# Low parts of 30 second feed-forward weight blocks: a DMA that adds the weights onto a negated high part, in place of VectorE's subtraction

## The reference, cut to what matters

```python
# first block, feed-forward part
h = rms_norm(x, g_pre_mlp[layer]) * (1.0 + scale2) + shift2
f = jnp.square(jax.nn.relu(h @ w_fc1[layer])) @ w_fc2[layer]
x = x + gate2 * rms_norm(f, g_post_mlp[layer])
# second block
for layer in range(DEPTH_2):
    hn = rms_norm_2(h, norm_g[layer])
    ...
    h = h + y.astype(h.dtype)
return rms_norm_2(h, final_g)
```

## Time and profile before

| what | value |
|---|---|
| median of 3 runs | 1418.52 us (1418.33 to 1418.89) |
| profiled execution, device time | 1419.24 us |
| profiled execution, span | 1417.4 us |
| TensorE busy | 1401.6 us, 99% of the span |
| VectorE busy | 948.4 us, 67% |
| ScalarE busy | 606.8 us, 43% |
| GpSimd busy | 0.2 us |
| moved by DMA | 157.99 MB, mean 111 GB/s |

### The profile page before, as it was taken

How to read it: one execution, slowest core, us unless ns; L and a number is a source line. 1 busy time by engine, 2 the same in 40 slices (tenths; PEclk the granted TensorE clock), 3 DMA queues, 4 the chain that set the end, 5 groups by cost and what they waited for, 6 DMA issues and landing times.

```text
span 1417.4 us, 21825 instructions
## 1 busy us (share of the span) xinstructions
PE 1401.6 (99%) x8618; PEld 1195.4 (84%) x8618; DVE 948.4 (67%) x1886; ACT 606.8 (43%) x1176; POOL 0.2 (0%) x4
## 2 busy tenths in 40 slices
PE   8999989999999999999999999999999999999998
PEld 7888878999998888888888888888888888888886
DVE  7887777789963335756466535422788889888645
ACT  6423345555542324542332333433445545556441
POOL 0000000000000000000000000000000000000000
PEclk9999999999999999999999999999999999999999
DMA  9656453233332324022332233132222222221221
GB/s 352 221 186 251 156 198 116 75 106 119 104 120 92 102 92 161 31 104 90 104 104 74 94 116 134 60 104 89 75 91 74 91 76 75 76 75 61 76 75 60
DMA packets 43734, 157.99 MB, mean 111 GB/s; under 512 B 4849, under 2 KB 5233, under 8 KB 43633
## 3 DMA queue, kind: packets, MB, share of 16 engines
q1 hardware_dynamic: 43344, 156.39, 32.4%
q10 hardware_dynamic: 288, 0.21, 0.0%
HBM read 154.48 MB, written 2.10 MB: 110 GB/s over the span
## 4 chain that ended last, share of the span: by engine, by line
PE 96%; DVE 2%; DMA 1%; issue 0%; ACT 0%; SPq 0%; DVEq 0%; ACTq 0%
PE PS L584 27%; PE PS L586 27%; PE PS L585 27%; PE PS L925 3%; PE PS L927 3%; PE PS L926 3%; PE PS L1056 1%; PE PS L580 1%; PE PS L1060 1%; PE PS L1048 1%; PE PS L988 1%; DMA RAW<-in_ada 1%; PE PS L1069 0%; DMA X<-in_x 0%; PE PS L1041 0%
## 5 line engine op out<-in xcount | busy, mean ns | idle before, releaser
L584 PE MATMUL PS<-HH,WH 128*128 128x512 f32 (+1 forms) x880 | 340.6, 387 | 0.0
L586 PE MATMUL PS<-HH,WL 128*128 128x512 f32 (+1 forms) x880 | 336.1, 382 | 0.0
L585 PE MATMUL PS<-HL,WH 128*128 128x512 f32 (+1 forms) x880 | 336.0, 382 | 0.0
L2217 ACT ACTIVATE WH<-RAW 128x1024 fp32r<-128x1024 f32 x192 | 202.3, 1057 | 188.1 <-PE PS L586 129.5
L1279 DVE TENSOR_TENSOR WL<-RAW,WH 128x1024 fp32r<-128x1024 f32 x192 | 233.3, 1220 | 67.0 <-ACT WH L2217 66.7
L586 PEld LDWEIGHTS PS<-HH,WL 128*128 128x128 f32 x880 | 165.5, 188 | 32.7
L584 PEld LDWEIGHTS PS<-HH,WH 128*128 128x128 f32 x880 | 165.6, 188 | 31.9
L585 PEld LDWEIGHTS PS<-HL,WH 128*128 128x128 f32 x880 | 165.6, 188 | 30.4
L584 PE MATMUL PS<-WH,ZH 128*128 128x512 f32 x400 | 156.3, 391 | 3.9 <-DVE Z L1593 2.1
L585 PE MATMUL PS<-WL,ZH 128*128 128x512 f32 x400 | 155.7, 389 | 0.0
L586 PE MATMUL PS<-WH,ZL 128*128 128x512 f32 x400 | 155.7, 389 | 0.0
(11 more groups left out here) (322 smaller groups left out, 2348.0 us busy)
## 6 DMA issues: line engine op xcount, KB each, us to landing
RAW<-in_w_fc SPq DMA_DIRECT2D x64, 512.0 KB, 3.3
RAW<-in_hgrn_in SPq DMA_DIRECT2D x64, 512.0 KB, 3.2
RAW<-in_ada SPq DMA_DIRECT2D x44, 512.0 KB, 4.5
RAW<-in_pool_in SPq DMA_DIRECT2D x40, 512.0 KB, 3.3
RAW<-in_w_in SPq DMA_DIRECT2D x26, 512.0 KB, 4.8
RAW<-in_pool_out SPq DMA_DIRECT2D x16, 512.0 KB, 3.3
RAW<-in_hgrn_out SPq DMA_DIRECT2D x16, 512.0 KB, 3.2
RAW<-in_w_out SPq DMA_DIRECT2D x8, 512.0 KB, 4.5
```

Of the source, the lines that this page charges most:

```text
L584: e.matmul(out, wh, xh, start=first, stop=False)
L585: e.matmul(out, wh, xl, start=False, stop=False)
L586: return e.matmul(out, wl, xh, start=False, stop=last)
L2217: e.activation(place(s)[0], raw(i), ACT.Copy).then_inc(whi.sem, whi(s))
```

## The change

For the 30 units of `w_fc2` that lie in the ring of four (k = 0 to 29; k = 30 and 31 lie in `ZR` and are as before), the low part is made in another way:

- ScalarE, after the high part, writes a second output from the same raw data: the copy with scale -1 into the place of the low part. It is the negated high part.
- GpSimd waits for that and issues a DMA that reads the same 512 KB of weights from main memory once more and adds them onto the place of the low part. What stands there then is raw minus high, as before, though not rounded to the shorter format by an engine.
- The DMA's end raises one of four new semaphores `s_added`, one for each place of the ring. TensorE waits for it in place of `taken`.
- SyncE's load into the raw buffer that such a unit leaves waits for ScalarE's second output in place of VectorE's low part.
- VectorE's 30 subtractions are gone.

```diff
+def low_list():
+    out, seen = {}, {}
+    for s, i in enumerate(GEMM):
+        if UNITS[i][0] == "w_fc2" and SLOT[s] < NS:
+            seen[SLOT[s]] = seen.get(SLOT[s], 0) + 16
+            out[s] = seen[SLOT[s]]
+    return out
+
+ADDED = low_list()
...
+        s_added = [sem(f"s_added{i}") for i in range(NS)]
...
+        def weights(s):
+            if s in ADDED:
+                return s_added[SLOT[s]], ADDED[s]
+            return taken.sem, taken.of(GEMM[s])
+
+        def split(i):
+            if UNITS[i][2] and GEMM.index(i) in ADDED:
+                return whi.sem, whi.of("minus", GEMM.index(i))
+            return taken.sem, taken.of(i)
...
-                    e.wait_ge(taken.sem, taken.of(RBEFORE[i]))
+                    e.wait_ge(*split(RBEFORE[i]))
...
-                e.wait_ge(taken.sem, taken.of(GEMM[s]))
+                e.wait_ge(*weights(s))
...
-                    if SLOT[s] is None:
+                    if SLOT[s] is None or s in ADDED:
                         continue
...
                     e.activation(place(s)[0], raw(i), ACT.Copy).then_inc(whi.sem, whi(s))
+                    if s in ADDED:
+                        e.activation(place(s)[1], raw(i), ACT.Copy, scale=-1.0).then_inc(whi.sem, whi("minus", s))
...
+        def pool_program(e):
+            for s in ADDED:
+                name, n, _ = UNITS[GEMM[s]]
+                e.wait_ge(whi.sem, whi.of("minus", s))
+                e.dma_start(out=place(s)[1], in_=a[name][n], accum_op=ALU.add).then_inc(s_added[SLOT[s]], 16)
```

More of the change, by code:

```diff
@@ L2895, in _ @@
             vector_program(e)
+        @block.gpsimd
+        def _(e):
+            pool_program(e)
         @block.scalar
```

## The result

The changed kernel takes 1436.33 us (median of 4 runs, 1434.28 to 1437.26) against 1418.7 us before (4 runs, 1418.33 to 1419.05): slower by 17.6 us, ratio 1.0122, 95% interval 1.0105 to 1.014. Its profiled execution took 1436.11 us with a span of 1434.1, 16.7 us longer than the span of before.

What follows compares the result with a forecast made beforehand. TensorE was taken as the bound, so lightening VectorE gains nothing; two uncovered DMA waits, 2 x 6.4 - 4.4 = 8.4 us, plus 0 for the clock, on 1418.5 us gave 1427.0 us, with an 8-in-10 range of 1420.5 to 1441.5 us.

Steps and rivals of the forecast that it cites:

- the two places: Start of the second feed-forward product (k = 0) and its end (k = 29, with k = 28), where TensorE would stop.
- the form of the sum: Cost is L less the cover at each end of the stage: (L - 3.14) + (L - 1.28) us.
- The covers: Time from TensorE wanting a unit back to its negated copy's end: 3.14 us start, 13.5 middle, 1.28 end.
- L: Time from the negated copy's end until TensorE may start on the unit; taken as 6.4 us.
- 0.95 us of queue: Each added negated copy occupies ScalarE's queue for 0.95 us, 28.5 us over 30; ScalarE does not become the bound.
- 2L - 4.4: Cost of the added wait at the stage's start and end together, 8.4 us with L = 6.4.
- The first two terms: Within L: 3.2 us for a plain load's landing, plus 1.6 us for the addition reading the destination.
- The rival built on the plain load's rows: Addition lands like a plain load, L from 3.2 to 3.6 us; 1420.5 to 1421.3 us, within 0.2%; chance 0.11.
- the rival of a slow but steady addition: L from 9 to 13.7 us, only the two stops show, long ones; 1432 to 1441.5 us; chance 0.17.
- the clock at 0: Lower granted clock behind the two stops might add 0 to 3 us; 0 taken, 3 kept for the range.
- stops of 3.3 and 5.1 us: Predicted TensorE waits at the start (k = 0) and the end (k = 29) of the second product.
- The rival of saturated DMA engines: An addition costs over 3.8 us of all sixteen engines, so the middle stalls as well; 1448 us; chance 0.08.

Runs made afterwards that it cites:

- the held-back load: Against the changed kernel, SyncE's load into a raw buffer waits until the addition of the unit that left it has landed; 1430.19 us.
- the copy: Against the changed kernel, the GpSimd DMA copies the weights over the negated high part and adds nothing; 1428.15 us (one run).

## Why the prediction was wrong

It said slower by 8.4 us, and 17.6 were measured: the direction, the two places and the form of the sum were right, and the size was off by a factor of two.

**Right.** TensorE bounds the stage, and a lighter VectorE gives nothing: shown by the kernel with only k = 1 to 25 added, 1419.79 us. The covers: 3.14 us at the start came out as 3.0, L of 9.99 us less the 6.98 by which the way to k = 0 grew (8.52 - 1.54). At the end the negated copy of k = 29 ended at 565.40 (564.36 + 1.04) and the unit started at 573.83, L = 8.43 us, which with the cover of 1.28 us makes 7.15; measured were 7.14. No wait appeared in the middle. ScalarE's second copy took its 0.95 us of queue at both places and delayed nobody else. Line 1746's wait was expected to be worth at most 0.6 us; it was worth 0.1 (0.64 to 0.52), as the second sum now waits 0.92 us for TensorE's own product.

**Wrong: L.** The step that failed is "L = 3.2 + 1.6 + 1.6 = 6.4 us". It was 10.0 us at the start and 8.4 at the end, which makes 2L - 4.4 into 18.4 - 4.4 = 14.0 us. The first two terms together were nearly right, 4.8 us against 5.3 for an addition by itself. What was mis-sized most is what the traffic beside it adds: 1.6 us against 4.3 at k = 0 (9.6 - 5.3):

| term | predicted | measured |
|---|---|---|
| base, by a copy | 3.2 | by itself not run; by GpSimd's path 4.3 at the least, beside a load, and 0.3 until it issues |
| the addition | 1.6 | base and addition 5.3 by themselves, for 4.8; in the stage's traffic 3.1 over a copy (7.7 - 4.6) |
| the load that starts with it | 1.6 | 2.8 (8.1 - 5.3), a second load among it |
| the next addition and load | not in the sum | 0.9 at the start (9.0 - 8.1), 1.5 with all others (9.6 - 8.1, where 9.1 to 10.0 were seen) |

The 1.6 us of engine time per 512 KB was measured well: the addition costs 2.9 us of the engines, the load 1.5. What failed was to take engine time for waiting time. The load is served first and the addition pays the whole overlap, and the next load comes while it is still under way, which had no term either. Why the load is served first isn't settled by these runs. That two units' additions follow each other by 1.9 us at the start stood in the order lists and in the earlier trace rows, and had no term. Without the loads it would have cost little: 5.5 us with the addition of k = 1 behind it, 5.3 without.

The Trainium skill (DMA: Bandwidth & Descriptors, Anatomy of one DMA — SWDGE (gpsimd) path) gives an estimate of 3.2 us for such a copy. Here a copy took 4.3 us at the least, but always beside a load, so no run here shows whether that holds for a copy by itself. The rival built on the plain load's rows, no measurable change, fell by the runs: an addition by itself took 5.3 us, and that alone cost 2.5 us of stop at k = 0.

The measured time lies where the rival of a slow but steady addition put it (L from 9 to 13.7, 1432 to 1441.5 us, chance 0.17): the mean of the two L is 9.2, and only the two places show stops. Its reason, that GpSimd is slow to make descriptors, did not hold. GpSimd issued 0.3 us after the copy's end, and a copy by the same path took 4.6 us in the median.

**Wrong: the clock at 0.** It was kept for the range only, up to 3 us. It cost 2.0 us from k = 0 to k = 26 and about 1.5 behind k = 29, 3.5 us. 14.0 + 3.5 is 17.5, less the 0.8 us by which this execution was ahead at the last half-size product, nearly all of it chance, makes 16.7, the difference of the two spans. The sum had stops of 3.3 and 5.1 us in it. Those of 5.31 and 6.83 us at k = 0 were followed by a clock of 0.90 and 0.80 in 413 to 430 us. Shorter ones went either way: 2.67 us (the held-back load) and 2.27 us (the copy) 0.90, 2.50 us (k = 0 alone, nothing beside it) 1.00. So already stops as long as those of the forecast had the clock in doubt, and a likeliest value of 0 was the low end of what the earlier trace rows showed. The Trainium skill (TensorE: Matmul & The Clock Gate, HAM oscillation — how this bites in real kernels) has waits for DMA slow the work behind them. The trace agrees at the 6.83 us stop, about 7.5 us for the unit k = 0 in place of 5.4.

The rival of saturated DMA engines did not happen: an addition took 2.9 us of the engines and not over 3.8, and at 0.87 busy no wait stood in the middle.

## What to carry to other kernels

When work moves from an engine to a DMA, look for the unit with the least time between being made and being used, at the first unit of a stage and where a loop changes its order, and not at the mean: 25 of 30 units could be moved for nothing, the other five cost 17 us. Size a DMA on a bounding path by its landing beside whatever the same event releases, here 8.1 to 10 us and not 5.3, and add what a stop of TensorE costs behind it in clock. And relieve an engine only where the bounding engine waits for it: 30 us less of VectorE bought nothing.

## What the runs showed of the hardware

- An addition by DMA of 512 KB onto on-chip memory takes 5.3 us from issue to landing by itself and 2.9 us of all sixteen engines, twice a copy. A copy by the same path, beside a load, takes 4.3 us at the least and 4.6 in the median (the addition 7.7), and 1.4 us of the engines. Reading the source from on-chip memory saved 0.6 us in the median.
- A load issued by SyncE and an addition issued by GpSimd at the same moment are not slowed alike: the load landed after 3.4 us, the addition after 8.1 in place of 5.3. From 411 to 412 us 86 packets of the load started and 4 of the addition.
- GpSimd's own instruction for the addition lasts 0.86 us, for a copy 0.53. With an area of 1024 for its descriptors it stood for 3.1 us before its fourth addition with no semaphore to wait for; with 2048 only the 1.0 us of waiting for ScalarE was left.
- The clock behind a stop of TensorE does not follow from the stop's length alone: 1.00 behind 2.50 us, 0.90 behind 2.27, 2.67 and 5.31, 0.80 behind 6.83 (means of 413 to 430 us). Behind 6.83 us it was at the lower level for some 4 us, which cost 2. With 27 thrown-away matmuls in the stop it stayed at 1.00.
